# A two-layer kernel on one core: the mean squares of attention heads as two products of split squares

## The reference, cut to what matters

```python
def rms_norm(x, g):
    xf = x.astype(jnp.float32)
    y = xf * lax.rsqrt(jnp.mean(xf * xf, axis=-1, keepdims=True) + EPS)
    return (y * g.astype(jnp.float32)).astype(x.dtype)
...
    q = rms_norm(q.reshape(b, s, N_Q_HEADS, HEAD_DIM), q_norm_g)
    k = rms_norm(k.reshape(b, s, N_KV_HEADS, HEAD_DIM), k_norm_g)
    v = v.reshape(b, s, N_KV_HEADS, HEAD_DIM)
    o = sliding_window_attention(q, k, v, sinks) * jax.nn.silu(z_a)
```

## Time and profile before

| | |
|---|---|
| median of three runs | 2475.81 us |
| the profiled execution | 2474.53 us |
| its span in the profile | 2472.8 us |
| PE busy | 2438.7 us, 99% of the span |
| DVE, ACT, POOL busy | 63%, 44%, 54% |
| granted TensorE clock | 1.0 of full in the whole run |
| first attention, pairs 0 to 6 | 34.27 us a pair |

### The profile page before, as it was taken

How to read it: one execution, slowest core, us unless ns; L and a number is a source line. 1 busy time by engine, 2 the same in 40 slices (tenths; PEclk the granted TensorE clock), 3 DMA queues, 4 the chain that set the end, 5 groups by cost and what they waited for, 6 DMA issues and landing times.

```text
span 2472.8 us, 36100 instructions
## 1 busy us (share of the span) xinstructions
PE 2438.7 (99%) x11658; PEld 2013.0 (81%) x11658; DVE 1552.9 (63%) x2240; ACT 1088.2 (44%) x2010; POOL 1325.5 (54%) x1092
## 2 busy tenths in 40 slices
PE   8999999999999999999999999999999999999999
PEld 5888888888788878888888888877788888878877
DVE  6555552343777776435666666756678777777785
ACT  4333333301666651126777777832433333344442
POOL 3798887443455554441111111254279888656683
PEclk9999999999999999999999999999999999999999
DMA  3222223579210015421111111431133333486652
GB/s 112 90 80 64 68 68 114 179 274 325 77 34 25 30 33 185 136 96 59 43 43 43 43 43 43 142 106 52 48 111 115 122 119 111 139 281 217 190 180 82
DMA packets 126498, 267.24 MB, mean 108 GB/s; under 512 B 13872, under 2 KB 14000, under 8 KB 126400
## 3 DMA queue, kind: packets, MB, share of 16 engines
q1 hardware_dynamic: 84800, 157.85, 20.1%
q10 hardware_dynamic: 41600, 108.19, 12.2%
HBM read 198.02 MB, written 67.96 MB: 108 GB/s over the span
## 4 chain that ended last, share of the span: by engine, by line
PE 89%; DVE 4%; ACT 2%; POOL 2%; issue 2%; DMA 1%; ACTq 0%; DVEq 0%; POOLq 0%
PE bank L804 20%; PE bank L1124 16%; PE bank L867 15%; PE flip L1124 8%; PE pv L1124 4%; PE flip L1292 4%; PE bank L1312 4%; PE pv L1292 4%; PE pv L1062 3%; PE score L1034 1%; PE score L804 1%; PE score L1031 1%; PE flip L1047 1%; PE pv L938 1%; PE bank L1047 1%
## 5 line engine op out<-in xcount | busy, mean ns | idle before, releaser
L639 POOL TENSOR_SCALAR whi<-raw 128x512 fp32r<-128x512 f32 x194 | 143.9, 742 | 780.4 <-PE bank L867 394.4
L641 POOL TENSOR_TENSOR wlo<-raw,whi 128x512 fp32r<-128x512 f32 x194 | 275.8, 1422 | 16.2
L804 PE MATMUL bank<-a_hi,whi 128*128 128x512 f32 x464 | 182.8, 394 | 2.1 <-issue 1.5
L804 PE MATMUL bank<-b_lo,whi 128*128 128x512 f32 x464 | 181.4, 391 | 0.0
L654 POOL TENSOR_TENSOR wlo<-a,whi 128x512 fp32r<-128x512 f32 x114 | 163.3, 1433 | 17.1 <-ACT whi L1688 16.9
L867 PE MATMUL bank<-b_hi,whi 128*128 128x512 f32 x384 | 156.4, 407 | 0.0
L867 PE MATMUL bank<-b_hi,wlo 128*128 128x512 f32 x384 | 150.7, 392 | 0.0
L867 PE MATMUL bank<-b_lo,whi 128*128 128x512 f32 x384 | 149.9, 390 | 0.0
L804 PE MATMUL bank<-b_hi,whi 128*128 128x512 f32 x336 | 131.6, 392 | 0.7 <-DVE b_lo L2303 0.4
L804 PE MATMUL bank<-a_hi,wlo 128*128 128x512 f32 x336 | 130.8, 389 | 0.0
L804 PE MATMUL bank<-a_lo,whi 128*128 128x512 f32 x336 | 130.8, 389 | 0.0
(11 more groups left out here) (710 smaller groups left out, 7619.8 us busy)
## 6 DMA issues: line engine op xcount, KB each, us to landing
raw<-in_w SPq DMA_DIRECT2D x206, 256.0 KB, 2.6
a<-in_pairs SPq DMA_DIRECT2D x152, 256.0 KB, 2.7
wd_scr<-wd SPq DMA_DIRECT2D x55, 256.0 KB, 4.9
wd<-in_down SPq DMA_DIRECT2D x44, 256.0 KB, 4.6
xs_scr<-made ACTq DMA_DIRECT2D x40, 256.0 KB, 2.6
fc<-c_scr ACTq DMA_DIRECT2D x16, 512.0 KB, 3.7
h_scr<-up_y ACTq DMA_DIRECT2D x13, 512.0 KB, 2.6
raw<-wd_scr SPq DMA_DIRECT2D x26, 256.0 KB, 2.9
```

Source lines behind the costliest of these rows:

```text
L639: nc.gpsimd.tensor_scalar(hi, src, 1.0, 1.0, ALU.mult, ALU.mult).then_inc(w_hi, 1)
L641: nc.gpsimd.tensor_tensor(lo, src, hi.bitcast(F32), ALU.subtract).then_inc(w_lo, 1)
L804: last = nc.tensor.matmul(psum_ap, ws[w][:, k, :], a[:, kt, hs(h)], start=(first and i == 0 and j == 0), stop=(final and i == n - 1 and j ...
```

## The change

`head_mean` is now fp32r, and the squares are split into a high and a low part, each an fp32r matmul with `head_mean` into the same sum. A half that was one fp32 matmul (two records in the trace, since the engine passes it twice) is now two fp32r matmuls. Who splits the squares: GpSimd both halves of the three early ones (behind the weight split of unit c+2) and half 0 in every pair (`square_parts`, between `window_parts(0)` and `window_parts(1)`); DVE half 1 in every pair (`square_parts`, between `maxima(3)` and `add(1)`). The wait of PE on the squares becomes one on the split squares.

In the pair PE takes half 0 behind `values(0)`, `flip_p(1)` and two steps of fill, and half 1 behind `flip_p(2)`. The scores of the next pair come one fill step (three matmuls) later, and their first two steps wait for half of the query's low parts only. ACT takes `log_mean(0)` behind `expo(2)`; its `log_mean(1)` stays ahead of `high(2)`. On GpSimd two more units are split ahead of the pairs; in a pair the split of the next first unit stands in two halves before and behind `window_parts(3)`, and the split of the unit after it ends the pair. The last pair has only one split instead of two. A semaphore is freed by letting an existing one (`prepared`) count on.

```diff
@@ GpSimd
+            def square_parts(n, h, parts, src, made):
+                hi, lo = (x[:, hs(h)] for x in parts)
+                pool.wait_ge(sw.q_sq, n * 2 + (h + 1))
+                settle()
+                nc.gpsimd.tensor_scalar(hi, src[:, hs(h)], 1.0, 1.0, ALU.mult, ALU.mult).then_inc(sq_parted, 1)
+                pool.wait_ge(sq_parted, made + 1)
+                settle()
+                nc.gpsimd.tensor_tensor(lo, src[:, hs(h)], hi.bitcast(F32), ALU.subtract).then_inc(sq_parted, 1)
...
+            for c in range(3):
+                split(U_SWA + 2 + c, (U_SWA + c) % 2, tile_done[1], U_SWA + 1 + c)
+                for h in range(2):
+                    square_parts(c, h, early_sq[c], early[2 * c + 1], 4 * c + 2 * h)
+            for u in range(U_PAIR, U_PAIR + 2):
+                split(u, u % 2, tile_done[1], u - 1)
...
                 window_parts(it, pp, 0)
-                split(u, 0, tile_done[1], u - 1)
+                if last_pair:
...
+                square_parts(n, 0, (sq_hi, sq_lo), s_sq, n * 2 + 6)
                 window_parts(it, pp, 1)
...
-                split(u + 1, 1, tile_done[1], u)
                 window_parts(it, pp, 2)
+                split(u, 1, tile_done[1], u - 1, (0,))
                 window_parts(it, pp, 3)
+                split(u, 1, tile_done[1], u - 1, (1,))
+                split(u + 1, 0, tile_done[1], u)
@@ TensorE
-            def mean_square(n, h, dst, square):
-                pe.wait_ge(sw.q_sq, n * 2 + (h + 1))
-                nc.tensor.matmul(dst, head_mean[:], square[:, hs(h)], start=True, stop=True).then_inc(sw.q_ms, 1)
+            def mean_square(h, dst, parts):
+                for m, x in enumerate(parts):
+                    last = nc.tensor.matmul(dst, head_mean[:], x[:, hs(h)], start=(m == 0), stop=(m == 1))
+                last.then_inc(sw.q_ms, 1)
...
                 values(1)
-                fill(1, 0, range(2))
-                pe.wait_ge(sw.exp, st * 4 + 12)
-                mean_square(n, 1, score[0][:, 0:HALF], s_sq)
-                fill(1, 0, range(2, 3))
+                fill(1, 0, range(3))
                 pe.wait_ge(sw.q_std, n * 2 + 1)
                 flip_p(2)
+                pe.wait_ge(sw.exp, st * 4 + 12)
+                pe.wait_ge(sw.q_n, n * 3 - 4)
+                mean_square(1, score[0][:, 0:HALF], (sq_hi, sq_lo))
                 fill(1, 0, range(3, KT))
                 values(2)
                 flip_p(3)
-                fill(1, 1, range(5))
+                fill(1, 1, range(6))
                 pe.wait_ge(sw.q_std, n * 2 + 2)
                 window_scores(*((it, 1) if pp == 0 else (it + 1, 0)), 0)
-                fill(1, 1, range(5, KT))
+                fill(1, 1, range(6, KT))
@@ ScalarE
                 query(0)
-                log_mean(flip[:], n, 0, s_sq)
                 fold(0)
                 high(1)
                 expo(2)
+                log_mean(flip[:], n, 0, s_sq)
@@ VectorE
+                def square_parts(n):
+                    dve.wait_ge(sw.q_sq, n * 2 + 2)
+                    settle()
+                    v.tensor_copy(sq_hi[:, hs(1)], s_sq[:, hs(1)]).then_inc(sw.q_n, 1)
+                    dve.wait_ge(sw.q_n, n * 3 - 5)
+                    v.tensor_tensor(sq_lo[:, hs(1)], s_sq[:, hs(1)], sq_hi[:, hs(1)].bitcast(F32), ALU.subtract).then_inc(sw.q_n, 1)
...
                 maxima(3)
+                square_parts(n)
                 add(1)
```

More of the change, by code:

```diff
@@ L970, in window_pair @@
                 fill(0, 1, range(2))
-                pe.wait_ge(sw.lo, st + 1)
-                mean_square(n, 0, flip[:], s_sq)
                 values(0)
                 flip_p(1)
-                fill(0, 1, range(2, 7))
+                fill(0, 1, range(2, 4))
+                pe.wait_ge(sw.lo, st + 1)
+                pe.wait_ge(sq_parted, n * 2 + 8)
+                mean_square(0, flip[:], (sq_hi, sq_lo))
+                fill(0, 1, range(4, 7))
                 scores(3)
```

53 lines of the change are left out of this document (29 added, 24 removed).

## The result

The changed kernel takes 2483.9 us in the median, against 2475.8 before: a ratio of 1.0036, 95% interval 1.0026 to 1.0045. Its profiled execution took 2485.0 us (span 2483.2), 10.4 us more of span than the one of before.

A forecast was written before the change was run, and what follows sets the result against it. PE, busy for 99% of the span, was taken as the bound. Pairs +9.1, early part -0.9 and last pair -0.9 gave +7.3 us on the profiled 2474.5, 2481.8; the median 1.3 above, 2483.1 us; range 2471.5 to 2488.5, likeliest case 2479 to 2488.

The forecast's parts named there:

- I would be wrong if those waits are absent: Sign: a pair's first fill waits for `s_z` about 1 us, some step 0 transposes for `sp`; pair 35.1 to 36.4 us.
- The walk: Step-by-step start times through one pair, from step 2's transposes to the pair's end, taken as good to 0.3 us.
- What PE saves: PE's mean squares: 0.40 us less for each of 20 halves, a ceiling of 8.0 us gained.
- Step 2: `high(2)` behind `log_mean(1)` comes only 0.1 us earlier; PE waits 1.1 us, not 0.40; seven pairs gain 0.8, not 5.6.
- The splits of squares are hidden: In a pair, DVE's and GpSimd's splits of squares finish before PE needs them; half 1 has 0.8 us of cover.
- The end of the pair: GpSimd's weight splits meet DVE's `neg_max` and `gated(1,0)`; with GpSimd first, `gate(1)` comes late and PE waits 1.05 us.
- rival A: DVE is first at the pair's end: 0 to +0.3 us a pair, 2474 to 2476, no change; chance 0.34.
- The next pair's transposes of step 0: DVE's TENSOR_TENSOR in `normalise(0)` may meet GpSimd's split and delay PE by 0 to 0.7 us; 0.35 a pair taken.
- The pair in sum: -0.12 + 1.05 + 0.35 = +1.3 us a pair, bounds +0.8 to +2.1; seven ends of pairs +9.1.
- Early part: Before the pairs: 1.6 us comes earlier, less what DVE loses beside GpSimd's twelve new operations; -0.9, between 0 and -1.6.
- Last pair: One split less, the one that made `neg_max` 0.9 us late; -0.9 us, between 0 and -1.2.

The follow-up runs named there:

- run 4: Kernel before with each mean square as two fp32r matmuls of squares that ACT writes rounded, nothing split or reordered; 2469.6 us, 0.9977.
- run 1: Kernel after with ACT's `log_mean` of half 1 moved behind `high(2)`; 2481.3 us, 1.0024.
- run 8: Kernel after in its order, without splits of squares: rounded squares, two matmuls each, in the pairs, fp32 early mean squares; 2480.4 us, 1.0021.
- run 9: Kernel after with GpSimd's weight splits as in before, half 0's squares ahead of the second, PE and ACT reordered, fp32 early, DVE's loop moved; 2479.6 us, 1.0020.
- run 10: Split squares in the order of before: DVE splits both halves, GpSimd as before, `high(2)` ahead of `log_mean(1)`, fp32 early, DVE's loop moved; 2474.5 us, 1.0001.
- run 2: Kernel after with GpSimd's whole weight split of the next pair's first unit back between the masks of steps 1 and 2; 2483.8 us, 1.0036.
- run 5: Kernel before with 22 satisfied waits (11 instructions) ahead of DVE's second-attention loop, placing it as in after; 2477.7 us, 1.0011.
- run 6: Kernel after with 220 satisfied waits (110 instructions) pushing DVE's second-attention loop on to 898 to 1259; 2481.7 us, 1.0028.
- run 3: Kernel after with the six early mean squares back in fp32 and GpSimd's loop over them left out; 2483.8 us, 1.0036.
- run 7: Kernel after with the edits of run 1, run 2 and run 3 together and DVE's loop moved by 110 instructions; 2476.3 us, 1.0007.
- run 11: Kernel before with each mean square as one fp32r matmul of rounded squares, no splits or reordering; 2466.2 us, 0.9967.
- run 12: Kernel before with one fp32r matmul of rounded squares per mean square and `high(2)` ahead of `log_mean(1)` on ACT; 2466.6 us, 0.9966.

## Why the prediction was right in its number, and where not in its steps

2483.1 us was forecast, slower; 2483.9 came, inside the range. That the number is so near is luck in part: the pairs cost 5.0 us where 9.1 were forecast, the early part and the last pair together cost 1.1 where a gain of 1.8 was, and a term that nobody had adds 3.0 in the trace. And by its own signs ("I would be wrong if those waits are absent") the forecast fails at the end of the pair: no wait for `s_z`, none for `sp` of step 0, and a pair of 35.02 us, just under the 35.1 to 36.4 given. The walk itself was close. With the 0.97 us by which the pair starts later added, its times are:

| | forecast | + 0.97 | measured |
|---|---|---|---|
| transposes of step 2 | 666.33 | 667.30 | 667.31 |
| `log_mean(1)` | 667.43 | 668.40 | 668.42 |
| `high(2)` | 668.1 | 669.1 | 669.00 |
| PE gets the last mask of step 2 | 672.3 | 673.3 | 673.19 |
| last mask of step 3 ends | 679.8 | 680.8 | 680.89 |
| TENSOR_TENSOR of the second half | 680.5 | 681.5 | 681.56 |
| `gated(1,0)` | 680.6 | 681.6 | 681.53 |

- **What PE saves.** Right. The records stand 0.23 apart in the early part, and run 4 gives 5.6 us in all with 4.7 of them in the seven pairs, against 0.8 x 7 = 5.6 of saved work there. Behind the transposes half 1 takes 0.55 (667.67 to 668.22) and not 0.46, but whatever stands there takes 0.09 more, in before the fill; the sum had it with the transposes (0.44).
- **Step 2.** Right, and shown by run 1. `high(2)` comes 1.69 behind the start of the transposes, forecast 1.77, and the wait is 0.97, forecast 1.1. Run 1 leaves 0.16 of it, so the rest is the order on ACT.
- **The splits of squares are hidden.** Right for where they stand, by run 8: 34.93 us a pair without them. In other places they were not hidden (runs 9 and 10). The copy of half 1 takes 0.43, within its bounds of 0.23 and 0.69.
- **The end of the pair.** Right up to the meeting: `normed_lo` held up by GpSimd's first half, masks of step 3 late by 0.9 us (0.8 forecast), slack of DVE's gate used up. The step that failed is what the meeting of `gated(1,0)` with the TENSOR_TENSOR does. "If GpSimd is first, it is held until about 681.6, `gate(1)` ends at 683.0, and PE waits 1.05 us": DVE was first by 0.03 us in every pair, which is rival A's condition, and that did not save PE. It was no toss of a coin either: `neg_max`, held by GpSimd's TENSOR_SCALAR, ends with it, and `gated` follows at once. The sum and rival A both left out that the first fill of a pair also waits for the low weights, and that these are what GpSimd makes there. 0.62 us were lost in the first pair, 0.71 on average with the slow first fill, not 1.05. Run 2, with the weights out of the way, shows the gate 0.41 late. What would happen with GpSimd first was not run.
- **The next pair's transposes of step 0** (0.35 a pair in the sum): nothing. DVE had `sp` ready at 686.4 and PE asked at 686.97. `neg_max` did take 0.80 instead of 0.23; PE's own loss of 0.62 had covered it. What did cost is what rival A has at 0 to 0.3, the split that runs into the masks of step 0: 0.1 to 0.2 us in most pairs and 0.9 in one.
- **The pair in sum**: +0.76 measured, +1.3 forecast with bounds of 0.8 and 2.1; over seven 5.0, not 9.1. This is the largest error of size.
- **Early part** (-0.9 forecast): the chain gained 0.14 us, not 0.9, since on DVE the norm of the queries stands behind the operations on `wd`, which lost 1.3 us beside GpSimd. The step that failed is the size of "what DVE loses beside GpSimd's twelve new operations": it was the split of weights that it met, not the squares. The pairs then start 1.0 us later than before (652.17 against 651.20), of which 0.56 go with the lower granted clock behind PE's longer wait (against run 2, see under hardware).
- **Last pair** (-0.9 forecast): nothing. After trails by 6.0 us at its start and by 6.1 at its end. PE waits 1.32 us for `sp` of step 1 where before has 0.29 for it and 0.53 for the gate behind it.
- **Missing**: the loop of DVE in the second attention, +3.1 us by run 5 and 1.1 to 2.2 by run 6. No rival had it, though the diff adds instructions to DVE's stream. Without it the kernel after would be near 2481 to 2482, an estimate from these two runs, and still in the range.

The trace of after reads +1.0 (early) + 5.0 (pairs) + 0.1 (rest up to the second attention) + 3.0 (loop) + 1.4 behind the loop = 10.5 (the spans differ by 10.47). The last is no more than the kernels of these series scatter behind it (their traces need 853 to 856 us from the last CUSTOM to the end, whatever the edit), and is left open. In the medians the difference is 8.1.

The Trainium skill (SBUF — State Buffer, Who interferes with whom) was cited for the hold between DVE and GpSimd. The traces agree with it both ways: GpSimd's TENSOR_TENSOR 1.81 us for 1.28 behind a DVE operation with two inputs, and DVE's 128x4 operation 0.61 (run 2) and 0.80 (after) for 0.23. By it the splits of squares could have cost something; in run 8 leaving them out gained nothing, so in the kernel after what they meet had slack.

## What to carry to other kernels

When an operation moves on the bounding engine, move its follower on the other engines too: here one line on ACT, left in its old place, was worth 2.0 to 2.6 us. Before calling a place the critical one, list everything that the waiting instruction waits for; removing the last releaser gains only its distance to the next (run 2 took away a wait of 0.44 us for the weights and left one of 0.41 for the gate). And compare code behind the change as well: a stall released by issue, at a loop's jump back, is a matter of where the code stands, and a pair of runs with padding tells it within one series.

## What the runs showed of the hardware

**Code that stands elsewhere.** With DVE's loop at 777 to 1138 or 898 to 1259 there is no stall and there are 49 or 50 packets of instructions of about 8 KB; at 788 to 1149 there are 59 packets and two stalls of 2.6 to 2.95 us at the two jumps back. The second attention is 3.0 us longer, about half of their 5.8 us. The Trainium skill (Runtime: NRT & Kernel Launch, Instruction fetch mechanics) states that a taken branch to a page outside of two that are held costs a fetch before execution goes on, with pages of 256 instructions. The two stalls stand at taken branches, as the rule has it. Its size of a page does not tell the three places apart: counted from the start of DVE's stream, 777 to 1138, 788 to 1149 and 898 to 1259 all lie in the same two pages of 256, and only one of them stalls. Which size would fit, and how many instructions stand ahead of the program's own, was not measured and stays open.

**Two engines that hold each other.** At the end of each of the seven pairs DVE's operation starts 0.03 us ahead of GpSimd's TENSOR_TENSOR, and it is GpSimd that is held: DVE takes 0.69 as in before, GpSimd 1.81 instead of 1.28. The operation ahead of it was the other way round: GpSimd's TENSOR_SCALAR takes its usual 0.62, and DVE's 128x4 operation beside it 0.32 instead of 0.23, up to 0.61 in run 2.

**The clock behind an idle PE.** In the kernel after PE is idle for 2.8 us ahead of 643.17, and the granted clock falls behind that; the windows from 643 to 646 and 646 to 649, PE's busy us and then its clock:

```profile
643.00:646.00 3.00, 2.83 (x16) 0.65 0.03 10
646.00:649.00 3.00, 3.00 (x17) 0.78 0.31 93
```

0.65 is a mix of the two levels of 2.4 and 1.2 GHz. From PE's transposes of the values (643.17 here) to the first pair, the kernels of this document need:

| kernels | PE idle ahead | lowest clock | us to the first pair |
|---|---|---|---|
| before, runs 5, 9, 10 | 0.5 to 0.8 | 1.00 | 7.87 to 7.88 |
| runs 3, 7, 8 | 0.5 to 0.7 | 1.00 | 8.03 to 8.14 |
| run 4 | 1.6 | 1.00 | 7.87 |
| run 11 | 2.1 | 1.00 | 7.87 |
| run 12 | 2.2 | 0.69 | 9.42 |
| run 2 | 2.8 | 1.00 | 8.44 |
| after, runs 6, 1 | 2.8 | 0.65, 0.54, 0.50 | 9.00, 9.37, 9.58 |

Runs 11 and 12 are alike up to there, as are after and runs 1, 2 and 6. So with the same code a fall of the clock goes with 1.55 us more (run 12) and with 0.6 to 1.1 (after, 6 and 1 against run 2). Of the 1.12 us by which after is slower here than before, 0.56 stay in run 2, where the clock did not fall; runs 3, 7 and 8, with the same splits of weights ahead of the pairs, have 0.15 to 0.26 of it. The start of the pairs scatters besides: 651.20 and 651.81 in before and run 5, which are alike up to there. PE's saved time turned into a wait, behind which the clock fell in four of six executions. Why it falls in one and not in the other stays open.
